# Recurrent stage of a hybrid decoder step: every gate tile one step ahead, the first in front of the first level

## The reference, cut to what matters

```python
qa, kva, ga, qb, fb, ib, gb, ma, mb = jnp.split(n @ w_in[l], splits, axis=-1)
o_b, s_new = hgrn2_mixer(qb, fb, ib, gb, lb[l], s0, hgrn_norm_g[l])
merged = jax.nn.sigmoid(ma) * (o_a @ w_branch_nsa[l]) + jax.nn.sigmoid(mb) * (o_b @ w_branch_hgrn[l])
...
def step(s, inp):
    b = jnp.cumsum(lc, axis=2)
    a = jnp.einsum('bhtk,bhsk,bhtsk->bhts', qc, kc, decay)
    o = jnp.einsum('bhtk,bhkv->bhtv', qc * jnp.exp(b), s) + jnp.einsum('bhts,bhsv->bhtv', a, vc)
    s = jnp.exp(b_last[:, :, 0, :, None]) * s + jnp.einsum('bhsk,bhsv->bhkv', kc * jnp.exp(b_last - b), vc)
```

## Time and profile before

| what | value |
|---|---|
| median of 3 runs | 3281.62 us (3279.41 to 3281.9) |
| profiled execution, its own time | 3281.45 us |
| its span, first to last instruction | 3279.7 us |
| mean granted TensorE clock | 0.941 |
| TensorE busy | 3015.7 us, 92% |
| VectorE busy | 1347.5 us, 41% |
| ScalarE busy | 964.3 us, 29% |
| recurrent stage, first layer | from 931.9 to about 1135 us of the span |
| recurrent stage, second layer | from 2525.8 to about 2729 us of the span |

### The profile page before, as it was taken

The page is one execution under the profiler, slowest core; times in us unless marked ns, Lnnn a source line. Parts: engine busy times, 40 slices in busy tenths (PEclk is TensorE's granted clock), DMA queues, the critical chain, the costliest instruction groups (busy, mean ns, idle before and its releaser), DMA issues. The chain is left out here.

```text
span 3279.7 us, 58783 instructions
## 1 busy us (share of the span) xinstructions
PE 3015.7 (92%) x24911; PEld 2855.5 (87%) x24911; DVE 1347.5 (41%) x2793; ACT 964.3 (29%) x1594; POOL 57.4 (2%) x32
## 2 busy tenths in 40 slices
PE   6999998989679898999989999888985998899997
PEld 4999998878469898999989999887873998899997
DVE  3332334356355454333343333443553635433334
ACT  2222222344243233222232222332443413322222
POOL 0000000000030000000000000000000300000000
PEclk7999999899889899999989999989997998899998
DMA  6746224431542335332256522263215425232331
GB/s 201 248 133 205 85 81 148 99 116 53 116 123 79 112 114 194 107 90 85 83 176 202 159 84 87 88 177 99 65 51 150 100 70 158 65 90 85 91 89 62
DMA packets 523703, 378.65 MB, mean 115 GB/s; under 512 B 43058, under 2 KB 469448, under 8 KB 522131
## 3 DMA queue, kind: packets, MB, share of 16 engines
q1 hardware_dynamic: 490068, 303.10, 32.3%
q10 hardware_dynamic: 33376, 71.83, 6.4%
HBM read 344.10 MB, written 39.07 MB: 117 GB/s over the span
## 5 line engine op out<-in xcount | busy, mean ns | idle before, releaser
L192 DVE TENSOR_TENSOR w_lo<-w_raw,w_hi 128x1024 fp32r<-128x1024 f32 (+1 forms) x390 | 480.8, 1233 | 1096.8 <-ACT w_hi L187 1096.6
L187 ACT ACTIVATE w_hi<-w_raw 128x1024 fp32r<-128x1024 f32 (+1 forms) x390 | 405.7, 1041 | 1312.6 <-PE pa L204 681.0
L204 PE MATMUL pa<-nhi,w_hi 128*128 128x272 f32 x1408 | 297.6, 293 | 29.1 <-DVE nlo L247 27.3
L204 PE MATMUL pa<-nhi,w_lo 128*128 128x272 f32 x1408 | 293.1, 290 | 0.0
L204 PE MATMUL pa<-ghi,w_hi 128*128 128x272 f32 x1408 | 291.4, 288 | 1.3 <-DVE glo L794 1.3
L204 PE MATMUL pg<-nhi,w_lo 128*128 128x272 f32 x1408 | 292.5, 289 | 0.0
L204 PE MATMUL pa<-nlo,w_hi 128*128 128x272 f32 x1408 | 292.5, 289 | 0.0
L204 PE MATMUL pg<-nhi,w_hi 128*128 128x272 f32 x1408 | 292.3, 289 | 0.0
L204 PE MATMUL pg<-nlo,w_hi 128*128 128x272 f32 x1408 | 291.5, 289 | 0.0
L204 PE MATMUL pa<-ghi,w_lo 128*128 128x272 f32 x1408 | 291.4, 288 | 0.0
L204 PE MATMUL pa<-glo,w_hi 128*128 128x272 f32 x1408 | 290.2, 288 | 0.0
(11 more groups left out here) (351 smaller groups left out, 4611.4 us busy)
## 6 DMA issues: line engine op xcount, KB each, us to landing
w_raw<-in_ffn_w_in SPq DMA_DIRECT2D x352, 192.0 KB, 2.8
ada_raw<-in_ada_w ACTq DMA_DIRECT2D x26, 2048.0 KB, 9.8
w_raw<-in_w_in SPq DMA_DIRECT2D x156, 192.0 KB, 3.0
w_raw<-in_ffn_w_out SPq DMA_DIRECT2D x128, 192.0 KB, 2.7
w_raw<-in_ffn_w_in SPq DMA_DIRECT2D x176, 128.0 KB, 2.9
ada_raw<-in_ada_w SPq DMA_DIRECT2D x10, 2048.0 KB, 15.3
w_raw<-in_ffn_w_out SPq DMA_DIRECT2D x160, 128.0 KB, 2.4
w_raw<-in_w_in SPq DMA_DIRECT2D x94, 128.0 KB, 3.1
```

The source lines that it names most:

```text
L187: act.activation(self.hi[slot][:, 0:k, :], self.raw[slot][:, 0:k, :], ACT.Copy).then_inc(self.hi_done, 1)
L192: dve.tensor_tensor(self.lo[slot][:, 0:k, :], self.raw[slot][:, 0:k, :], self.hi[slot][:, 0:k, :].bitcast(F32), ALU.subtract).then_inc(sel ...
L204: mm = pe.matmul(out[:, half, 0:HALF], w[slot][:, k0 + n, :], x[:, n, half * HALF:(half + 1) * HALF], start=(n == 0 and w is self.hi and x ...
```

## The change

Tile 0 is multiplied before anything else of the stage, and each later half gate stands where the half of one tile further on stood: `half_gate(2 * pos + 2)` in place of `half_gate(2 * pos)` and so on, so that the last two of the eight updates have no half gate behind them. The parks and splits of ScalarE and the splits of VectorE are moved by one tile with them. SyncE's and GpSimd's programs are as before. Nothing is added or taken away on any engine.

```diff
@@ scalar
                         act.activation(d, bc[:, :, :] if n == NL else d, ACT.Exp).then_inc(e_done, 1)
-                        if n >= 1:
-                            park(n - 1)
+                        park(n)
...
-                    park(8)
                     park(9)
+                    park(10)
...
-                            park(9 + t // 2)
+                            park(10 + t // 2)
...
-                    for i in range(12, NG):
+                    for i in range(13, NG):
@@ vector
                         select(ORDER[pos])
-                        if n >= 1:
-                            wt.split_lo(dve, wt.at(n + 1), DC)
+                        wt.split_lo(dve, wt.at(n + 2), DC)
                     select(NL - 1)
-                    wt.split_lo(dve, wt.at(8), DC)
+                    wt.split_lo(dve, wt.at(9), DC)
...
-                        if b % 2 == 1 and 14 + b // 2 < len(tiles_):
-                            wt.split_lo(dve, wt.at(14 + b // 2), DC)
+                        if b % 2 == 1 and 15 + b // 2 < len(tiles_):
+                            wt.split_lo(dve, wt.at(15 + b // 2), DC)
@@ tensor
+                    half_gate(0)
+                    half_gate(1)
                     turn_input(0)
...
-                        half_gate(2 * pos)
+                        half_gate(2 * pos + 2)
                         if 1 <= pos < 5:
                             turn_input(pos)
-                        half_gate(2 * pos + 1)
+                        half_gate(2 * pos + 3)
...
-                            half_gate(16 + t)
+                            half_gate(18 + t)
...
-                            half_gate(20 + t)
+                            half_gate(22 + t)
...
-                        half_gate(24 + b)
+                        if 26 + b < 2 * NG:
+                            half_gate(26 + b)
```

More of the change, by code:

```diff
@@ L1865, in _ @@
                     dve.tensor_tensor(pj[:, 4:8, :], k, pj[:, 0:4, :], ALU.mult).then_inc(qe_done, 1)
-                    wt.split_lo(dve, wt.at(9), DC)
+                    wt.split_lo(dve, wt.at(10), DC)
                     dve.wait_ge(qe_done, 2)
@@ L1872, in _ @@
                         if t in (2, 4):
-                            wt.split_lo(dve, wt.at(9 + t // 2), DC)
+                            wt.split_lo(dve, wt.at(10 + t // 2), DC)
                     for t in range(4):
@@ L1884, in _ @@
                         if t in (1, 3):
-                            wt.split_lo(dve, wt.at(12 + t // 2), DC)
+                            wt.split_lo(dve, wt.at(13 + t // 2), DC)
                     dve.wait_ge(sin, 32)
```

## The result

The changed kernel takes 3293.51 us (median of 6 runs, 3290.55 to 3299.37); the kernel before, run beside it, 3279.09 us (3272.91 to 3281.90). The ratio is 1.0046, with a 95% interval of 1.0035 to 1.0057: slower by 11 to 19 us, where 15.7 us were forecast. The profiled execution took 3295.97 us.

What follows compares the result with a forecast made beforehand. TensorE, busy 92% of the span, was taken as the bound; 2.5 us at the start, 7.5 for the end's wait and 5.7 for the clock there sum to 15.7 us slower, 3297.2 us. The 8-in-10 range was 3288 to 3303.

Steps and rivals of the forecast that it cites:

- the start: Stage start: later first gate product plus four transposes in the dense stretch, 1.67 and 0.87 us, 2.5 us together.
- The first gate product at nlo's landing: Sign at the stage's start: first gate product waits for nlo, 14 us after the start, TensorE idle before it.
- the clock changes nothing here: Stage start: about 5 us at the lower clock fall on the gates instead of the first level, no net effect.
- The end's wait: Stage end: column sums wait for VectorE until 5.9 us after the last gate product; net 3.75 us per layer, 7.5 in all.
- TensorE's last update is done before VectorE wants it: Stage end: the eighth update starts about 3.3 us after the last gate product and takes 1.15 us.
- The clock at the end: Stage end: column sums run at 1.2 GHz nearly throughout, 7.1 us long, 2.85 us more, 5.7 us in both layers.
- The factor of 1.84: Price of the lower clock for the column sums, from L1995's 16 narrow products: 1.95 us against 3.58 us.
- The same waits follow there: Middle of the stage up to the last updates: TensorE meets the same waits, nothing won, cost put at nothing.
- The clock holds: Rival at the stage's end: full clock through the column sums; 10.0 us slower, 3291.5 us; chance 0.19.
- not slower: Rival at the start: gates start well before nlo's landing; 4.1 us more, or 1.6 us less than now; chance 0.08.
- The gates warm TensorE: Rival at the start: first level's gain from the higher clock won in full; 10.6 us slower, 3292.1 us; chance 0.09.
- Dearer: Rival: tile 2's landing pushed back, TensorE idle 5 us in each layer; 25.7 us slower, 3307.2 us; chance 0.07.

Runs made afterwards that it cites:

- e2: Kernel before, with gate tile 0 alone put in front of the first level; 3277.7 us, ratio 0.9993 to the kernel before.
- e3: The change, with VectorE's low split of the last weight tile moved behind the eighth update's addition; 3285.2 us, ratio 1.0025 to the kernel before.
- e5: The change, with the first two of the eight updates without half gates in place of the last two; 3280.8 us, ratio 1.0005 to the kernel before.
- c0: The kernel before, unchanged, profiled once more; 3276.4 us in one run.
- e8: e5 with tile 0's products by nhi first, behind a wait for nhi's load alone; 3278.1 us, ratio 0.9994 to the kernel before.
- e4: e2 with tile 0's products by nhi first, behind a wait for nhi's load alone; 3283.2 us, ratio 1.0006 to the kernel before.
- e12: e8 with SyncE's load of tile 2's raw data moved in front of the samples' states; 3270.7 us, ratio 0.9975 to the kernel before.
- e10: Kernel before, with the norm moved in front of the last gates and the states' stores ahead of the last gate's; 3281.0 us, ratio 1.0003.
- e13: e12 with norm and stores moved as in e10, and VectorE's tile 9 split and queries' product behind the keys' product; 3275.9 us, ratio 0.9989.

## Why the prediction was right, and where it was not

Its mechanism held at both ends: the first gate product waits for nlo, VectorE's queue holds the column sums, and the clock falls before them. That the median came within 1.3 us of the forecast is partly luck: measured on the two profiles its terms are 17.7 us, 3.8 at the start and 13.9 at the end, against 15.7.

- **The first gate product at nlo's landing**: right, 14.65 and 14.37 us after the issue. The start cost 2.0 and 1.8 us, where 1.67 and 0.87 were put; e2, e3 and e5 show 0 to 1.8, and the runs of e2 leave 1.3 us at most for both layers, so a price of 2.5 us for the start is not shown. The statement "the clock changes nothing here" was too strong. The bounds of this term do not follow from their conditions (0.35 us twice is 0.7 and not 0.9, two more in each layer give 6.5 and not 5), and the row that it took for a level at the full clock is of narrower products; the level itself takes 4.11 us against 4.05.
- **The end's wait**: right in mechanism and size (H + 6.31 and 6.04 against 5.9), and e3 shows that 3 us of it hang on the split. That TensorE's last update is done before VectorE wants it did not hold in the first layer, where it ran at the lower clock.
- **The clock at the end**: right in size; the fall came at H + 2.6 and H + 4.6, where H + 4.4 to 6.3 was put. The factor of 1.84 taken from the samples' outputs against 7.47 / 3.97 = 1.88. H to end grew by 9.67 and 8.84 us; less 2.3 us for the earlier H that is 7.4 and 6.5 us, 13.9 in both, against the forecast's 13.2 for the wait and the clock together. The ratios of the change and of e5 (1.0046 and 1.0005) give about as much, 13 us.
- **"The same waits follow there"**: right for the waits, not for the clock behind them. In the changed kernel's profile it fell in the first layer's samples' outputs (some 2.2 us there and 0.7 in the updates) and behind the second layer's 2.58 us wait (1.3 us, less 0.2 us in the rest of that stage). These 4.0 us, with 3.8 and 13.9, make up the 21.7; but c0 shows such falls in the kernel before too, so they are not to be counted as a price of the change.
- **The rivals.** *The clock holds* and *not slower* fell by the rows of the end and of the start. *The gates warm TensorE*: the first level does get its 2.5 us, and the gates pay them. The advice of the Trainium skill to warm TensorE up first (TensorE: Matmul & The Clock Gate, "Why this matters for your kernels"; it is given there for measuring matmuls) was no gain here, where the warming work is on the path itself. *Dearer* did not come: tile 2's split ran at 956.40 and TensorE did not wait for it; e8 shows it binding once the start is earlier.

What stays open: by the profiles the change costs some 17 to 22 us, by the runs 11 to 19; one profile a kernel does not settle the difference. Nor is it shown what the start alone costs in the runs, or why the clock falls behind a wait in one stage and not behind the same wait in another.

## What to carry to other kernels

When an operation moves forward in one engine's order, look at what its last pieces leave uncovered at the other end, and which waits in another engine's queue stood in their shade: one split in front of two small operations cost some 4 us a layer (H to end in the change and in e3), about twice what the start lost. A gap of TensorE is worth its length plus what the clock does behind it, so closing one gap may open a dearer one: e4 won 2.6 us and lost 5, e12 closed the following ones and won. Where TensorE was the bound (e10, e13), products moved among its other products were not hidden.

## What was not expected of the hardware

Two stages of the same kernel, with the same waits, differ by over 2 us (203.2 to 205.6), and what differs in their rows is the granted clock: behind the same 2.58 us of idle TensorE it fell to 1.2 GHz in 14 of 24 stages and held in 10. Behind 1.86 us (e4) it fell for some 10 us; the loss there, near 5 us besides the gap itself, was more than twice the gap.
